# Turn, copy and product moved within the twelve attention steps of a fused three-layer model kernel

## The reference

```python
def hybrid_mixer(h, ...):
    u = h @ w_in
    y_a = short_conv_mixer(...)          # gated convolution
    y_n = nsa_mixer(...)                 # sparse attention: 8 heads, 2 key groups, 64 wide
    y_g = gated_deltanet_mixer(...)
    branches = einsum('bsrc,rcd->bsrd', stack([y_a, y_n, y_g]), w_branch)
    gates = sigmoid(h @ w_gate + b_gate).reshape(b, s, 3, dm)
    return sum(gates * branches, axis=2) @ w_out
# nsa_mixer, for each head: three softmaxes, each times its own gate and its own values
#   s_c: queries x 15 compressed keys      -> o_c
#   s_s: queries x selected keys (at 256 tokens all four blocks are selected) -> o_s
#   s_w: queries x window of 512 (here all earlier keys)                      -> o_w
#   o = g0 * o_c + g1 * o_s + g2 * o_w
```

## Time and profile before

| what | value |
|---|---|
| median of 3 runs | 2071.38 us (2068.4 to 2072.27) |
| the profiled execution, its own time | 2071.38 us |
| its span, first to last instruction | 2069.4 us |
| PE busy | 1848.0 us, 89% of the span |
| DVE busy | 1007.8 us, 49% |
| ACT busy | 661.4 us, 32% |
| TensorE's mean granted clock | 0.952 |
| first to last attention slot (48 to 71) | 1354.0 to 1496.2 us |

### The profile page before, as it was taken

The page is one execution under the profiler, slowest core; times in us unless marked ns, Lnnn a source line. Parts: engine busy times, 40 slices in busy tenths (PEclk is TensorE's granted clock), DMA queues, the critical chain, the costliest instruction groups (busy, mean ns, idle before and its releaser), DMA issues.

```text
span 2069.4 us, 30789 instructions
## 1 busy us (share of the span) xinstructions
PE 1848.0 (89%) x12687; PEld 1525.2 (74%) x12687; DVE 1007.8 (49%) x1404; ACT 661.4 (32%) x941; POOL 21.6 (1%) x14
## 2 busy tenths in 40 slices
PE   5999948999799978969998899987786999999998
PEld 3999938999699976769997799876674444444444
DVE  2978478886684445264445776455423111111111
ACT  3434314433444424244444533444411000000000
POOL 0000000000000000000000111000000000000000
PEclk8999979999899999989998999999996999999999
DMA  9989406987285421335441323422232999999996
GB/s 399 372 329 333 180 31 260 348 337 273 84 343 183 182 82 62 122 140 183 182 182 45 123 96 116 186 96 89 92 122 80 419 426 425 426 426 427 426 426 282
DMA packets 44582, 483.04 MB, mean 233 GB/s; under 512 B 4944, under 2 KB 5200, under 8 KB 5200
## 3 DMA queue, kind: packets, MB, share of 16 engines
q1 hardware_dynamic: 44352, 480.74, 59.0%
q10 hardware_dynamic: 144, 1.05, 0.1%
HBM read 480.72 MB, written 1.05 MB: 233 GB/s over the span
## 4 chain that ended last, share of the span: by engine, by line
PE 74%; DVE 10%; DMA 10%; ACT 4%; issue 1%; SPq 0%; DVEq 0%; ACTq 0%
PE psG L361 42%; PE psA L361 22%; DMA ring<-stream 9%; PE psS L361 8%; DVE rstd L1725 1%; DVE parts L1972 1%; DMA X<-x_in 1%; DVE mem L1764 1%; DVE H L1735 1%; ACT parts L1404 1%; ACT mem L1571 1%; DVE parts L1696 0%; DVE mem L1987 0%; DVE mem L2254 0%; DVE X L1773 0%
## 5 line engine op out<-in xcount | busy, mean ns | idle before, releaser
L361 PE MATMUL psG<-parts 128*128 128x256 f32 x6016 | 785.7, 291 | 71.1 <-DVE parts L1750 34.3
L361 PEld LDWEIGHTS psG<-parts 128*128 128x128 f32 x6016 | 762.7, 199 | 82.4 <-issue 75.7
L361 PE MATMUL psA<-parts 128*128 128x256 f32 x2112 | 267.2, 283 | 0.0
L1696 DVE TENSOR_TENSOR parts<-ring,parts 128x2048 fp32r<-128x2048 f32 x88 | 201.4, 2289 | 121.7 <-ACT parts L1272 121.6
L361 PEld LDWEIGHTS psA<-parts 128*128 128x128 f32 x2112 | 259.4, 192 | 0.3 <-issue 0.3
L361 PE MATMUL psS<-ring,mem 128*64 128x512 f32 (+1 forms) x1032 | 229.6, 594 | 13.6 <-DMA ring<-stream 11.9
L1272 ACT ACTIVATE parts<-ring 128x2048 fp32r<-128x2048 f32 x88 | 168.1, 1911 | 102.2 <-PE psA L361 102.0
L361 PEld LDWEIGHTS psS<-ring,mem 128*64 128x64 f32 (+1 forms) x1032 | 72.5, 137 | 166.3 <-issue 130.4
L1972 DVE TENSOR_TENSOR parts<-ring,parts 128x1024 fp32r<-128x1024 f32 x76 | 95.2, 1258 | 113.3 <-ACT parts L1404 112.4
L1687 DVE SCALAR_TENSOR_TENSOR mem<-ring,silc,mem 128x1536 f32<-128x1536 f32 (+1 forms) x98 | 138.9, 1417 | 2.7 <-issue 0.2
L1619 ACT ACTIVATE mem<-psS 128x512 f32<-128x512 f32 x16 | 9.6, 597 | 369.0 <-PE psS L361 369.0
(11 more groups left out here) (318 smaller groups left out, 1417.7 us busy)
## 6 DMA issues: line engine op xcount, KB each, us to landing
ring<-stream SPq DMA_DIRECT2D x304, 1536.0 KB, 8.6
X<-x_in SPq DMA_DIRECT2D x1, 1024.0 KB, 17.5
mem<-masks ACTq DMA_DIRECT2D x1, 1024.0 KB, 4.8
x_out<-X SPq DMA_DIRECT2D x1, 1024.0 KB, 3.9
cst<-consts SPq DMA_DIRECT2D x1, 240.0 KB, 2.9
cols<-cols_in SPq DMA_DIRECT2D x1, 224.0 KB, 2.5
```

The source lines that it names most:

```text
L361: return nc.tensor.matmul(out, lhsT, rhs, start=start, stop=stop, skip_group_check=True)
L1696: V.tensor_tensor(WG[f % 2][:, 1, :], chunk(c, 0, 2 * SLOT), WG[f % 2][:, 0, :], ALU.subtract).then_inc(sem("lo_gu"), 1)
```

## The change

In each round p of the loop the order becomes:

| engine | before | after |
|---|---|---|
| PE | fill(48+2p), scores(p+2), product(p-1), fill(49+2p), turn(p) | fill(48+2p), turn(p), scores(p+2), fill(49+2p), product(p) |
| ACT | tick(48+2p), soft(p+1), outcome, tick(49+2p), copy(p) | tick(48+2p), soft(p+1), copy(p), tick(49+2p), outcome |
| DVE | tick(48+2p), scaled(p), largest(p+1), tick(49+2p), outcome_low | tick(48+2p), outcome_low, scaled(p), largest(p+1), tick(49+2p) |

`outcome(t)` follows the third product of its head at once, no longer one round later; `outcome_low(t)` comes a little after it. Behind the loop, `turn(11)` and `copy(11)` go ahead of slot 70, `product(11)` ahead of slot 71, and both outcomes of the last head ahead of tick 71. No instruction is added or taken away.

```diff
@@ PE
                 for p in range(11):
                     fill(48 + 2 * p)
+                    turn(p)
                     if p + 2 < 12:
                         scores(p + 2)
-                    if p:
-                        product(p - 1)
                     fill(49 + 2 * p)
-                    turn(p)
+                    product(p)
+                turn(11)
                 fill(70)
-                product(10)
-                turn(11)
+                product(11)
                 fill(71)
-                product(11)
@@ ACT
                     soft(p + 1)
-                    if p and p % 3 == 0:
-                        outcome(p // 3 - 1)
+                    copy(p)
                     tick(49 + 2 * p)
                     if 49 + 2 * p == 59:
                         sigmoids(2, 59)
-                    copy(p)
+                    if p % 3 == 2:
+                        outcome(p // 3)
+                copy(11)
                 tick(70)
-                copy(11)
+                outcome(3)
                 tick(71)
-                outcome(3)
@@ DVE
                     tick(48 + 2 * p)
+                    if p and p % 3 == 0:
+                        outcome_low(p // 3 - 1)
                     scaled(p)
                     largest(p + 1)
                     tick(49 + 2 * p)
-                    if p and p % 3 == 0:
-                        outcome_low(p // 3 - 1)
                 scaled(11)
                 tick(70)
-                tick(71)
                 outcome_low(3)
-                for s in range(72, NFILL):
+                for s in range(71, NFILL):
                     tick(s)
```

## The result

| | time |
|---|---|
| changed kernel, median of 4 runs | 2103.99 us (2100.72 to 2105.8) |
| kernel before, median of 4 runs | 2070.2 us |
| ratio, with 95% interval | 1.0158 [1.0146, 1.0172] |
| span of the profiled execution | 2099.9 us, was 2069.4 |

The change makes the kernel slower by 1.6%, 33.8 us between the medians of four. The ratio takes in all 15 runs of the changed kernel, whose median is 2102.77 us; by it the loss is 32.7 us. The forecast was slower, by 23 us.

A forecast was written before the change was run, and what follows sets the result against it. The attention rounds' chain of waits through ACT and DVE was taken as the bound, its losses reaching the end. Queues 20.3 plus clock 2.8 made 23.1 us lost on 2071.4: 2094.5, own range 2085 to 2102, overall 2080 to 2103.

The forecast's parts named there:

- What bounds the rounds: Attention rounds: a chain of waits through ACT and DVE, PE idle once per round; a us lost there delays the end.
- The turn's place: Each round: turn waits for scaled, 4.15 behind the even slot; odd slot ends at 8.65 to 8.95, before about 4.2.
- copy and product: Each round: copy adds 0.79 on ACT before the odd slot's move-out, product 0.8 on PE before the next even slot.
- The sum of the queues: Cost of the new call order in all rounds and behind the loop: 8.8 + 3.2 + 8.65 - 0.4 = 20.3 us lost.
- the part behind the loop: From slot 70 to slot 72, behind the loop: 12.0 against 12.4 us, a gain of 0.4.
- The clock, net 2.8 lost: Low clock in the rounds: 10.6 us come back before even slots, 13.4 are paid on scores and odd slots.
- the price of 1.33 per pause: Low clock's mean cost over the kernel before's eight pauses ahead of slots, 10.6 us in all, charged to the new pauses.
- Rival 2: Each round's turn prolongs the low clock: 4.4 us in all, 2098.9; or for a whole round, 2111; chance 0.08.
- Rival 1: Clock stays up after the new pauses in the rounds: 20.3 - 10.6, so 2081.1; chance 0.09.
- Rivals 3 and 4: 3: faster, turn in the rounds not late, 2063.6, chance 0.05. 4: rounds don't decide, experts catch up, 2071, chance 0.04.

The follow-up runs named there:

- the turn put back: Changed kernel with turn(p) on PE again behind the odd slot, ahead of product(p): 2094.18 us, ratio 1.0115.
- The two warm kernels: Changed kernel and kernel before, each with idle-time matmuls added on PE in its pauses, results unread: 2081.83 us and 2061.61 us.
- the warm changed kernel: Changed kernel with idle-time matmuls between fill(48+2p) and turn(p) and ahead of turn(11), results unread: 2081.83 us, ratio 1.0056.
- scores first: Changed kernel with scores(p+2) ahead of turn(p) on PE: 2088.52 us.
- the turn alone: Kernel before with only turn(p) moved on PE, to right behind fill(48+2p): 2111.29 us, ratio 1.0202.

## Why the prediction was right, and where its size was off

- What bounds the rounds, and that a loss there reaches the end: right. The experts' stage kept its pace, and the attention stage's 35.4 us (180.8 - 145.4), less 1.5 in slots 72 to 75 and some 3 elsewhere, are the span's 30.5.
- The turn's place: right. The turn waits 4.17 us for scaled (forecast about 4.1), and scores and odd slot with it. Moved alone it costs 40 us, the low clock included.
- copy and product: right in kind. Shown by the turn put back, 23 us slower than the kernel before (some 10 of them the clock's, by the count), and by the even slot behind product in its chain. That the branch rounds are the dearest for them is not shown apart from the clock: in that kernel they took 2.0 to 2.9 us longer than in the kernel before, the gate rounds 0.7 to 2.6.
- The sum of the queues, 20.3: right in size. The two warm kernels differ by 20.2 us, and by 21.6 once the low stretches left in them are taken out. Nearly all that 20.3 lacks of it is the part behind the loop, 1.35 too cheap, where slot 70's slow run was counted twice.
- The clock, net 2.8 lost: this term was mis-sized. What comes back was nearly right (10.6 forecast; 9.2 measured with two stretches left, so some 12.2 at 1.5 for each). What is paid was forecast at 13.4; the warm changed kernel gives 22.2, and one stretch was left in it, so some 23.7. That is net 11.5 lost, and with the queues' 21.6 it makes 33.1 of the 33.8 us. The step that failed is the price of 1.33 per pause, taken over from pauses in front of a slot. With the pause in front of turn and scores a low stretch lasted 6.8 us in eight of eleven rounds.
- Why 6.8 us has two answers. In rounds 1, 4 and 7, scores of 15 columns stood between turn and slot; a stretch with turn in their place lasted 3.4 us in scores first. In rounds 0, 2, 5 and 8 the fall came 1.4 to 2.3 us before the turn, inside the pause. In the kernel before that happened once in seven, at slot 50. The prediction priced neither. How often a fall comes inside the pause can be partly luck, and no run settles it.
- Rival 2 had the mechanism in part: it let the low clock last longer, but put it on the turn. The time measured lies between its two cases, 2098.9 and 2111, 5 us above the first. The rule of the Trainium skill in "TensorE: Matmul & The Clock Gate", Part 4: PE-mode transpose, that a transpose doesn't count as busy time in the same way, is not borne out as the cause here: with the scores moved behind the odd slot, the turn still stood right behind each pause, and nine of eleven stretches lasted 3.4 us.
- Rival 1 (clock stays up, 2081) is near what the warm kernel measured, 2081.8, but only by added work. Rivals 3 and 4 fell.

What stays open is which property of the scores (64x128 weights, 15 columns in some rounds) matters. They were moved, not changed in shape; in the two rounds of the changed kernel where PE was busy nearly throughout with scores of 256 and 128 columns (3 and 9), the stretch lasted 3.4 us, which points to the 15 columns.

## What to carry to other kernels

When an instruction is moved ahead on an in-order engine, find when its input is ready at the new place, and charge the wait to everything queued behind it; for the rounds of the loop this came out within 0.1 us by adding up rows. Then look at what the first work behind the new pause is: here it ran at the low clock, and on the chain, and the price taken from pauses in another place was 10 us too low. And before moving the waiting instruction, ask what stands ahead of its producer: here two calls on DVE in another order gave 28 us, where the change lost 34.

## What the runs showed of the hardware that was not expected

Low stretches in these kernels lasted 3.4, 6.8 or 10.2 us. Those that began on a slot of dense matmuls were over after 3.4 us, six times of six in the kernel before. Where PE did turn, scores of 15 columns and slot without a break, they lasted 6.8 (rounds 1, 4 and 7 of the changed kernel). They lasted 6.8 too in round 2 of the changed kernel, where the stretch began 1.4 us before the turn, and 10.2 in round 4 of the turn alone, where it began 1.2 us before. The transposes of a turn ran at either clock: 0.88 us at 1.00, 1.54 at 0.50. Idle-time matmuls in the pauses were worth 22 us in the changed kernel, whose pauses were mostly 3.8 to 4.8 us long, and 9 us in the kernel before.
